# Layer 0 of a two-part model on one Trainium2 core: another way to decode the chosen positions, and an earlier turn and earlier gates

## The reference, cut to what matters

```python
def peer_ffn(h, w_query, sub_keys, expert_u, expert_v):
    q = (t @ w_query).reshape(t_count, PEER_HEADS, 2, PEER_HALF)      # 8 heads, 2 halves of 128
    s = jnp.einsum('thpd,hpkd->thpk', q, sub_keys).astype(F32)        # 128 keys per half
    s1, i1 = lax.top_k(s[:, :, 0], PEER_TOPK)                         # 16 of 128
    s2, i2 = lax.top_k(s[:, :, 1], PEER_TOPK)
    cand_s = (s1[..., :, None] + s2[..., None, :]).reshape(..., 256)
    cand_i = (i1[..., :, None] * N_KEYS + i2[..., None, :]).reshape(..., 256)
    top_s, pos = lax.top_k(cand_s, PEER_TOPK)                         # 16 of 256
    idx = jnp.take_along_axis(cand_i, pos, axis=-1)                   # the experts, 8 x 16 a token
    gate = jax.nn.softmax(top_s, axis=-1)
    act = gelu(expert_u[idx] . t) * gate                              # 16384 experts
    out = sum(act * expert_v[idx])
```

## Time and profile before

| | before |
|---|---|
| median of 3 runs | 3640.57 us (3635.67 to 3642.06) |
| the profiled execution | 3633.79 us, span 3632.5 us |
| PE busy | 3406.7 us (94%) |
| DVE busy | 2777.4 us (76%) |
| POOL busy | 1517.4 us (42%) |
| ACT busy | 1621.9 us (45%) |
| mean granted clock of PE | 0.968 |

### The profile page before, as it was taken

One profiled execution on the slowest core, in us unless ns is written; L12 is line 12 of the kernel. 1 busy time (PEld: TensorE's weight loads), 2 busy tenths in 40 slices (PEclk: granted clock), 3 DMA queues, 4 the chain that ended last, 5 costly groups with the idle time before them and its releaser, 6 DMA issues.

```text
span 3632.5 us, 59739 instructions
## 1 busy us (share of the span) xinstructions
PE 3406.7 (94%) x23981; PEld 3182.1 (88%) x23981; DVE 2777.4 (76%) x4937; ACT 1621.9 (45%) x2520; POOL 1517.4 (42%) x820
## 2 busy tenths in 40 slices
PE   7998999999979999799999989999998999988899
PEld 4667998889979999799999977999998999877799
DVE  6867777458999999588888766887755777757585
ACT  3533444333325555333333345546663333458353
POOL 2665555234777787555555300776661000000000
PEclk8999999899989999899999989999999999998899
DMA  6442112323867999989999621577777888631365
GB/s 235 143 124 65 47 53 94 122 87 124 274 203 271 338 336 338 324 310 340 337 336 339 231 88 46 178 219 238 259 263 245 280 278 279 209 118 53 99 198 163
DMA packets 250083, 752.24 MB, mean 207 GB/s; under 512 B 24144, under 2 KB 101840, under 8 KB 242512
## 3 DMA queue, kind: packets, MB, share of 16 engines
q1 hardware_dynamic: 119808, 418.70, 35.9%
q10 hardware_dynamic: 93136, 195.49, 15.3%
q0 software_dynamic: 36864, 134.23, 9.8%
HBM read 661.82 MB, written 85.98 MB: 206 GB/s over the span
## 4 chain that ended last, share of the span: by engine, by line
PE 64%; DVE 15%; DMA 7%; POOL 4%; ACT 4%; issue 4%; ACTq 0%; DVEq 0%; POOLq 0%
PE ps L138 62%; DVE paone L80 3%; POOL lo L80 3%; DMA paGg<-paG 3%; DMA parow<-in_u_rows,paidx 2%; DVE n_sq L113 2%; PE ps L141 2%; DVE paR L80 2%; POOL cond L80 2%; ACT hi L133 1%; DVE lo L80 1%; DVE g_b L80 1%; DVE paav0l L80 1%; DMA paA<-paga 1%; DMA ring<-in_adas 0%
## 5 line engine op out<-in xcount | busy, mean ns | idle before, releaser
L80 POOL TENSOR_TENSOR lo<-ring,hi 128x1024 fp32r<-128x1024 f32 x392 | 956.4, 2445 | 961.4 <-ACT hi L133 960.2
L133 ACT ACTIVATE hi<-ring 128x1024 fp32r<-128x1024 f32 x725 | 768.2, 1060 | 764.1 <-PE ps L138 645.9
L80 DVE TENSOR_TENSOR lo<-ring,hi 128x1024 fp32r<-128x1024 f32 (+1 forms) x333 | 406.7, 1223 | 228.8 <-ACT hi L133 228.1
L138 PE MATMUL ps<-pahh,hi 128*128 128x384 f32 (+1 forms) x1152 | 408.2, 354 | 25.1 <-POOL lo L80 22.2
L138 PE MATMUL ps<-pahl,hi 128*128 128x384 f32 (+1 forms) x1152 | 397.4, 345 | 0.0
L138 PE MATMUL ps<-pahh,lo 128*128 128x384 f32 (+1 forms) x1152 | 397.4, 345 | 0.0
L138 PE MATMUL ps<-pchh,hi 128*128 128x256 f32 x1152 | 334.8, 291 | 14.1 <-POOL lo L80 12.3
L138 PE MATMUL ps<-pchl,hi 128*128 128x256 f32 x1152 | 327.1, 284 | 0.0
L138 PE MATMUL ps<-pchh,lo 128*128 128x256 f32 x1152 | 326.9, 284 | 0.0
L138 PEld LDWEIGHTS ps<-pahh,hi 128*128 128x128 f32 x1152 | 220.7, 192 | 32.7 <-POOL lo L80 24.9
L138 PE MATMUL ps<-g_b,g_b 128*128 128x128 f32 x1856 | 234.5, 280 | 12.8 <-ACT g_b L133 9.3
(11 more groups left out here) (489 smaller groups left out, 9749.5 us busy)
## 6 DMA issues: line engine op xcount, KB each, us to landing
ring<-in_u SPq DMA_DIRECT2D x256, 512.0 KB, 4.2
ring<-in_v SPq DMA_DIRECT2D x256, 512.0 KB, 4.7
ring<-in_adat SPq DMA_DIRECT2D x56, 512.0 KB, 3.6
paA<-paga ACTq DMA_DIRECT2D x128, 192.0 KB, 4.8
paG<-paR ACTq DMA_DIRECT2D x12, 2048.0 KB, 8.5
paAg<-paA ACTq DMA_DIRECT2D x16, 1536.0 KB, 8.6
paGg<-paG ACTq DMA_DIRECT2D x16, 1536.0 KB, 22.7
ring<-in_ffn_up SPq DMA_DIRECT2D x44, 512.0 KB, 3.7
```

What stands on the lines that cost most here:

```text
L80: return Op(self.e.tensor_tensor(out, a, b, op) if self.real else None)
L133: return Op(self.e.activation(out, a, ACT.Copy, scale=scale) if self.real else None)
L138: return Op(self.e.matmul(out, l, r, start=start, stop=stop, skip_group_check=skip) if self.real else None)
```

## The change

The decode works on bf16 pairs instead of fp32. A unit's buffer holds 16 x 128 one-hot numbers, position part outermost, as 2048 bf16; the comparison reads the parts and the numbers 0..15 (`kinds`) as pairs; the product multiplies by the indices, each stored twice (`ixd`, made by `doubled_indices`, two copies for each token tile, in place of one copy to fp32 for all); and four additions of halves (1024, 512, 256, 128 elements) replace the reduction. The steps are staggered by one each, so six units take eleven steps, with a dot behind the first eight as before. Eight buffers of half the size are used, six by the main decode. `turn_at` goes from 46 to 39, the gates start at tile 43 instead of 50, `spread` from four groups in three tiles to five in four, which moves the last group from tile 121 to 119 and `fetch` from 124 to 122. The due times of dots 18 to 25 go from 37 + j to 30 + j, and the exponential of the scores on ACT from tile 42 to 35. The due times of dots 0 to 17 stay.

```diff
-        eqs = [R[:, 2048 * i:2048 * i + 2048].rearrange("p (h k a) -> p h k a", h=8, k=16) for i in range(4)]
+        hots = [R[:, 1024 * i:1024 * i + 1024].bitcast(BF16) for i in range(8)]
-        ixf = R[:, 10240:11264].rearrange("p (t n k) -> p t n k", t=4, n=16)
+        ixd = R[:, 10240:11264].bitcast(BF16).rearrange("p (t q n) -> p t q n", t=4, q=2)
...
-        ap3 = [scr(128) for _ in range(2)]
+        row_no = scr(128)
+        ap3 = [scr(64).bitcast(BF16) for _ in range(2)]
...
+        kinds = scr(16).bitcast(BF16).rearrange("p (a two) -> p a two", two=2)
-        ap = [ix_[:, wd * q:wd * q + wd].rearrange("p (t h k) -> p t h k", t=nd, h=8) for q in range(2)]
+        ap = [ix_[:, wd // 2 * q:wd // 2 * q + wd // 2].bitcast(BF16) for q in range(2)]
...
-        turn_at, start = 46, 50
-        spread = (1, 1, 2)
+        turn_at, start = 39, 43
+        spread = (1, 1, 1, 2)
...
-                due_at[k] = 37 + j
+                due_at[k] = 30 + j
...
-                if i == 42:
+                if i == 35:
                     act.wait_ge(s_pick, (name, "shifted"))
...
+        def doubled_indices(t):
+            for q in range(2):
+                op = dve.cp(ixd[:, t, q].rearrange("p (a h two) -> p a h two", a=16, h=8),
+                            bc(ixu[:, t, q:16:2, :].rearrange("p h a -> p a h").unsqueeze(3), (128, 16, 8, 2)))
+            return op
...
-                dve.tt(buffers[j % nb].rearrange("p h k a -> p (h k) a"), bc(part_of(t, q).unsqueeze(2), (128, 128, 16)),
-                       bc(iota[:, 0:16].unsqueeze(1), (128, 128, 16)), ALU.is_equal).then_inc(s_pick, (name, tag, "eq", j))
+                dve.tt(buffers[j % nb].rearrange("p (a n two) -> p a n two", a=16, two=2),
+                       bc(part_of(t, q).rearrange("p (n two) -> p n two", two=2).unsqueeze(1), (128, 16, 64, 2)),
+                       bc(kinds.unsqueeze(2), (128, 16, 64, 2)), ALU.is_equal).then_inc(s_pick, (name, tag, "eq", j))
...
-                dve.tt(buffers[j % nb], buffers[j % nb], bc(ixf[:, t, q:16:2, :].unsqueeze(2), (128, 8, 16, 16)), MUL).then_inc(
-                    s_pick, (name, tag, "times", j))
+                dve.tt(x, x, bc(ixd[:, t, q].rearrange("p (n two) -> p n two", two=2).unsqueeze(2), (128, 128, 8, 2)),
+                       MUL).then_inc(s_pick, (name, tag, "half", j, 2048))
...
-                dve.red(to(t, q), buffers[j % nb].rearrange("p h k a -> p (h k) a"), ADD).then_inc(s_pick, (name, tag, "sel", j))
+                dve.wait_ge(s_pick, (name, tag, "half", j, 2 * n))
+                if n > 128:
+                    dve.tt(x[:, 0:n], x[:, 0:n], x[:, n:2 * n], ADD).then_inc(s_pick, (name, tag, "half", j, n))
+                else:
+                    dve.tt(to(t, q), x[:, 0:n], x[:, n:2 * n], ADD).then_inc(s_pick, (name, tag, "sel", j))
+            for step in range(len(units) + 5):
+                if step < len(units):
+                    equal(step)
+                if 0 <= step - 1 < len(units):
+                    times(step - 1)
+                for k, n in enumerate((1024, 512, 256, 128)):
+                    if 0 <= step - 2 - k < len(units):
+                        half(step - 2 - k, n)
+                if between and step < len(units) + 2:
+                    between(step)
```

More of the change, by code:

```diff
@@ L1851, in times @@
             def times(j):
                 t, q = units[j]
+                x = buffers[j % nb].rearrange("p (n k two) -> p n k two", n=128, two=2)
                 dve.wait_ge(s_pick, (name, tag, "eq", j))
-                dve.tt(buffers[j % nb], buffers[j % nb], bc(ixf[:, t, q:16:2, :].unsqueeze(2), (128, 8, 16, 16)), MUL).then_inc(
-                    s_pick, (name, tag, "times", j))
-            def total(j):
+                dve.tt(x, x, bc(ixd[:, t, q].rearrange("p (n two) -> p n two", two=2).unsqueeze(2), (128, 128, 8, 2)),
+                       MUL).then_inc(s_pick, (name, tag, "half", j, 2048))
@@ L1858, in total, with half @@
+            def half(j, n):
                 t, q = units[j]
-                dve.wait_ge(s_pick, (name, tag, "times", j))
-                dve.red(to(t, q), buffers[j % nb].rearrange("p h k a -> p (h k) a"), ADD).then_inc(s_pick, (name, tag, "sel", j))
[L1862 to L1870, removed]
+                x = buffers[j % nb]
+                dve.wait_ge(s_pick, (name, tag, "half", j, 2 * n))
[3 more added lines that the diff above has]
+                    dve.tt(to(t, q), x[:, 0:n], x[:, n:2 * n], ADD).then_inc(s_pick, (name, tag, "sel", j))
@@ L1885, in rows_chosen @@
             dve.cp(top3, x[:, :, 0]).then_inc(s_pick, (name, "top rows"))
-            dve.cp(ixf[:, T], ixu[:, T]).then_inc(s_pick, (name, "ixf rows"))
+            doubled_indices(T).then_inc(s_pick, (name, "ixf rows"))
             dve.wait_ge(s_pick, (name, "top rows"))
@@ L1889, in rows_chosen @@
             bits("rows", tiu[:, T].rearrange("p h k -> p (h k)"), abu[:, 0:128], ap3)
-            decode("rows", [(T, q) for q in range(2)], (eqs[0], eqs[3]), lambda t, q: ap3[q], lambda t, q: sel3[q])
-            dve.stt(ap3[0], sel3[0], 128.0, sel3[1], MUL, ADD).then_inc(s_pick, (name, "numbers"))
+            dve.wait_ge(s_pick, (name, "ixf rows"))
+            decode("rows", [(T, q) for q in range(2)], (hots[0], hots[6]), lambda t, q: ap3[q], lambda t, q: sel3[q])
+            dve.stt(row_no, sel3[0], 128.0, sel3[1], MUL, ADD).then_inc(s_pick, (name, "numbers"))
             dve.wait_ge(s_pick, (name, "numbers"))
-            dve.cp(sparse["idx"][:, :], ap3[0]).then_inc(s_pick, (name, "rows"))
+            dve.cp(sparse["idx"][:, :], row_no).then_inc(s_pick, (name, "rows"))
             softmax_sum("rows", (name, "rows"), x, sum3, sparse["gate"][:, :].rearrange("p (h k) -> p h k", h=8), 8).then_inc(
@@ L1897, in vector @@
         def vector():
-            dve.cp(iota_b.bitcast(BF16), iota).then_inc(s_pick, (name, "iota"))
+            dve.cp(iota_b.bitcast(BF16), iota)
+            dve.cp(kinds, bc(iota[:, 0:16].unsqueeze(2), (128, 16, 2))).then_inc(s_pick, (name, "iota"))
             for hh in range(8):
@@ L1908, in vector @@
             dve.cp(top, x[:, :, 0]).then_inc(s_pick, (name, "top"))
-            dve.cp(ixf[:, 0:nd], ixu[:, 0:nd]).then_inc(s_pick, (name, "ixf"))
+            for t in range(nd):
+                op = doubled_indices(t)
+            op.then_inc(s_pick, (name, "ixf"))
             dve.wait_ge(s_pick, (name, "top"))
@@ L1912, in vector @@
             dve.wait_ge(s_pick, (name, "ixf"))
[L1913 to L1916, removed]
+            bits("all", tiu[:, 0:nd].rearrange("p t h k -> p (t h k)"), abu, ap)
+            decode("all", [(t, q) for t in range(nd) for q in range(2)], hots[0:6],
+                   lambda t, q: ap[q][:, 128 * t:128 * t + 128],
                    lambda t, q: sel[q][:, t].rearrange("p h k -> p (h k)"), lambda j: [dot(k) for k in dots_unit[j]])
```

## The result

The changed kernel takes 3644.06 us (median of 22 runs), the kernel before 3636.89 us beside it (22 runs): a ratio of 1.0020, 95% interval 1.0011 to 1.0030. That is 7 us slower, where 2 us faster was forecast. (The median lies inside the range given, 3625 to 3650; the direction was wrong.) The profiled execution took 3642.62 us around a span of 3641.3 us, 8.8 more than the span of before. It lasted 663.6 us before (1524.84 - 861.20) and 672.9 after (1534.78 - 861.90): +9.2. A second execution of the unchanged kernel (the last experiment) gave 661.7, so by these two executions the stage repeats to about 2 us, and the time from its start to the transposes to 0.1.

What follows compares the result with a forecast made beforehand. PE's losses in layer 0's up half were taken as the bound. Earlier turn +29.1, earlier transposes -22.7, gates -7.4 and end -0.8 gave -1.8 us on the 3640.57 median: 3638.8, range 3625 to 3650.

Steps and rivals of the forecast that it cites:

- What bounds the kernel: Up half of layer 0's expert layer, us 861 to 1525: otherwise full of PE work, with time lost in places.
- two holes and their three sums: PE idle between 1000 and 1100 and at the stage's end; losses 30.2 us before transposes, 9.4 in gates, 20.1 at end.
- Prices of the instructions: New bf16 decode operations: 1.22 us for 2048 elements, 3.6 us a unit against 6.6; doubled indices +0.7 us.
- The rival of the fp32 pace: Paired bf16 operations run no faster than fp32: 3 us more a unit, kernel at 3652 us; chance 0.04.
- The decode of the rows: Two units decoded from 873.6: end near 890.5, 3 us earlier, of which 1.7 us lasts after head 2's dots.
- Heads 5 to 7: DVE's sums in these heads meet fewer low halves: 5.5 and 3.2 us won, so routing ends at 1004.9.
- The walk: Step-by-step timing of DVE and POOL through the main decode, dots 18 to 25, ending with transposes at 1060.
- D': Time at which the changed kernel's transposes start: 1060, bounds 1052 and 1070, against 1082.7 before.
- The bound of 1070: Latest start foreseen for the transposes, if no head's sum is freed and gathers take 2.76 us in every step.
- The gates and the end: Stretch of gate groups, then last tiles before the down half: -7.4 us (0 to -9.4) and -0.8 (+3 to -8.3).
- POOL and PE are starved: Rival: PE stands from 998.5 until 1016, returns at its low clock; turn at 1072, kernel 3651 us; chance 0.12.
- The rival that the locks dissolve: Head sums free and row 21 in time: transposes at 1052, 12 us gained, kernel 3628.8 us; chance 0.30.

Runs made afterwards that it cites:

- decoding alone: Changed decode with the schedule of the kernel before (turn at 46, gates from 50, due times 37+j); ratio to before 0.9989, median 3629.89 us.
- the last kernel: Schedule of before, bf16 comparison and product, contiguous reduction, parts stored twice, dots of heads 6 and 7 due at 32 and 36; ratio to before 0.9942.
- due times 37 + j: Changed kernel with only the due times of dots 18 to 25 put back from 30+j; ratio to before 1.0009, median 3637.73 us.

## Why the prediction was wrong

**What bounds the kernel: right.** The stage, its two holes and their three sums hold; the unchanged 4.16 a tile ends at the same tile 33. Only that PE moves at the dots' pace from tile 34 on was too broad: before, tiles 38 to 41 took 4.16 each. Span minus stage is 2968.9 before and 2968.4 after. That these two agree so well is luck, since it was 2972.2 when the kernel before was profiled again.

**Prices of the instructions: right.** 1.23 for 2048 elements, six casts of the doubled indices in 1.30, and 3.69 for a full step of a unit without POOL, where 3.6 was worked out. The rival of the fp32 pace fell.

**The decode of the rows, right in kind.** It ended at 888.5 (forecast 890.5), but head 2's dots then waited for their rows: 1.90, 2.93 and 2.86 us. Of the 1.7 expected there 0.4 was left.

**Heads 5 to 7, nearly.** Their sums took 3.52, 2.30 and 0.76 for 13.7 before: 7.1 won, forecast 8.7. With the 1.3 missing at head 2 routing ended at 1008.5, 2.9 later than forecast. The shift was free (0.35), as argued, since POOL stood before gather 24 for 18.1 us; the first comparison came 3.3 after routing (3.9 forecast). But the shift reads one operand only, as the casts of the doubled indices do, so the prediction's rule that an instruction with two SBUF operands waits doesn't cover it. The casts, priced at 1.2 us or 2.5, took 1.30 here and 8.71 in "decoding alone", where three low halves stood beside them.

**The walk, the step that failed.** D' was put at 1060 and was 1071.4; in the stage's own time -12.1 us for -22.7. This is the term that was mis-sized, and it went wrong at five places, which give the 11.4 between 1060 and 1071.4:

- the first comparison, +2.9: routing's end +2.9 and the stage's own start +0.7, less 0.7 behind routing
- the step before dot 20: POOL had its second low half begun within it, so that three operations took 6.15; +2.0
- the wait for row 21: 6.8 us for 4.8, with DVE ready 3.5 later than assumed and the row's dot 7.5 after the issue of its gather; as less was lost in the next step, +0.3. The cause was named right, and moving the gather took the wait away
- the step before dot 25: four halvings met a low half (4.27 for 1.42); +2.9
- the tail: two low halves in a row, 4.63 long, stood beside six small halvings that take 1.42 alone: 6.52, where the walk had 2.7 with one low half; +3.7, less 0.4 for the last product, which was free.

So the lock was the right mechanism and too small a sum: it was left out of the step before dot 25, and counted once in the tail, where POOL has no dot to hold it and does two low halves in a row. The bound of 1070 was worked out for other causes and was passed by 1.4.

**The gates and the end, right in sign.** -5.9 for -7.4 and -2.6 for -0.8. Five groups in four tiles made PE nearly the bound: 65 of the 77 tiles take 4.9 or 5.65 us, and PE's matmuls wait 2.8 us for DVE's gate products, 7.3 before. DVE still waits 19.7 us for rows there (21.7 before). Of the 5.9, 1.3 is tile 121 of the first profile of before, which its second didn't repeat. The block of ACT comes behind tile 122 (21.4 us for 22.6).

**The rivals.** That POOL and PE are starved came nearest in time: a turn 10.7 us later than in the forecast costs what it said. But its mechanism decided little: tile 39 ended at 1062.3 (1061.6 on the clock of before, whose stage began 0.7 earlier), no later than the turn from which by the forecast the kernel would lose (1061.8), and PE then waited 9.1 us for DVE. PE's starving is a consequence; DVE set the turn, by the locks and the wait for row 21. The rival that the locks dissolve was held likeliest after the forecast, and is refuted by the same rows.

Summed in the stage: 10.6 of the error are the turn's, 1.5 the gates', 0.8 the tiles between, and -1.8 the end's: 11.1 for the 11.0 between -1.8 and +9.2.

Whether the last product is free was foretold by none of the sums, but the timelines show where the difference lies. Behind the decoding's last gather POOL makes two low halves in a row. With halvings this pair stands beside the last of them (6.52 us), and the product takes 0.56 (after and three experiments); with a reduction it stands beside the product, which takes 5.47 to 5.68 (before and five experiments).

What stays open: why tile 121 takes 6.2 us in some executions and 4.9 in others, and what the contiguous reduction would give with the early turn, which no experiment ran.

## What to carry to other kernels

Do the count of work behind a synchronization point first: while another engine sets the moment of the turn, each tile by which the turn is moved ahead costs its full time (4.16 us here), and the setting engine has to come earlier by as much. Cheaper instructions are worth their saving only if they keep their freedom from the neighbour's lock: four halvings with the bf16 operations saved 3 us of work a unit and gave 2.2 to 2.9 back for each low half, where the reduction they replaced cost more work and no lock. Once an engine's lock is priced, walk it through the tail too, where nothing else holds the neighbour back, and measure up to the event that others wait for: a collision that leaves one instruction can come back in the next.

## What the runs showed of the hardware

- A reduction of 2048 bf16 elements to 128 takes 2.27 us with its 16 elements side by side, the same as fp32 (2.275), and 3.6 to 3.9 with them 256 bytes apart.
- A comparison with one operand in PSUM takes 1.21 or 1.22 us whatever POOL does; with both in SBUF, 1.23 alone and 3.31 beside a low half (in the last kernel). The Trainium skill (SBUF — State Buffer, Who interferes with whom) says that a vector instruction with two inputs in SBUF contends with an instruction of GpSimd that reads SBUF, and that copies, casts and tensor_scalar can contend too, with one input, in modes that use both ports. The traces agree on both: the shift (a tensor_scalar) took 7.67 us for 0.35, six casts 8.71 for 1.30.
- An indirect DMA's issue is held too: 0.95 us beside a comparison from PSUM, 1.7 beside the same one with two SBUF operands, 2.76 beside the fp32 one.
- Three low halves in a row (7.0 us) held one small operation on DVE for all their length (7.67 for 0.35), and two held the last product (5.68 for 0.56). That isn't so each time: with due times 37 + j three low halves took 10.09 us beside comparisons and products (timeline of POOL below), and each of the three was held itself (3.4 us for 2.4) while DVE's operations got in between them. In the first two cases a gather stood right before the run, in the third none did; whether that decides it no run shows.

```profile
1017.09 10.09 POOL L80 TENSOR_TENSOR lo<-ring,hi 128x1024 fp32r<-128x1024 f32 x3 [2.21 <-ACT hi L133]
```
